# A differential-attention prompt stage on one core: score banks in turns, row maxima issued ahead of the merge

## The reference

```python
s = jnp.einsum("bqhd,bkhd->bhqk", q, k).astype(F32) * (DA_QK ** -0.5)
s = jnp.where(k_pos[None, :] <= q_pos[:, None], s, -jnp.inf)
p = jax.nn.softmax(s, axis=-1).reshape(b, DA_HEADS, 2, tq, tk)
w = p[:, :, 0] - lam * p[:, :, 1]
return jnp.einsum("bhqk,bkhd->bqhd", w.astype(v.dtype), v)
```

## Time and profile before

| | us |
|---|---|
| median of 3 runs (lowest, highest) | 2958.01 (2953.16, 2962.52) |
| the profiled execution's own time | 2952.79 |
| span of its core | 2951.1 |
| attention, from the first scores to the last output | 1342.6 to 1575 |
| PE busy, share of the span | 93% |
| DVE, ACT busy, share of the span | 46%, 22% |
| mean granted clock of PE over the span | 0.957 |

### The profile page before, as it was taken

One profiled execution on the slowest core, in us unless ns is written; L12 is line 12 of the kernel. 1 busy time (PEld: TensorE's weight loads), 2 busy tenths in 40 slices (PEclk: granted clock), 3 DMA queues, 4 the chain that ended last, 5 costly groups with the idle time before them and its releaser, 6 DMA issues.

```text
span 2951.1 us, 51413 instructions
## 1 busy us (share of the span) xinstructions
PE 2745.0 (93%) x21313; PEld 2582.2 (87%) x21313; DVE 1361.3 (46%) x1339; ACT 658.3 (22%) x967; POOL 257.1 (9%) x250
## 2 busy tenths in 40 slices
PE   6999999999999999996776999669999999999998
PEld 6999999999999999993344889439999999999998
DVE  4332233233673788776553656475453322332334
ACT  4111111112311222323322232111221111111123
POOL 1000000000000232111002454100000000000000
PEclk8999999999999999997987999769999999999999
DMA  3111111111333456669534000104211111111112
GB/s 101 50 43 50 43 50 50 43 43 50 115 99 103 143 175 223 201 188 330 164 114 124 25 28 17 42 29 145 92 44 50 50 43 45 48 50 45 48 41 74
DMA packets 270203, 252.02 MB, mean 85 GB/s; under 512 B 20724, under 2 KB 216144, under 8 KB 269920
## 3 DMA queue, kind: packets, MB, share of 16 engines
q1 hardware_dynamic: 252960, 189.42, 21.5%
q0 software_dynamic: 16896, 60.33, 5.6%
q10 hardware_dynamic: 192, 0.07, 0.0%
HBM read 209.87 MB, written 39.90 MB: 85 GB/s over the span
## 4 chain that ended last, share of the span: by engine, by line
PE 85%; DVE 9%; ACT 2%; issue 1%; DMA 1%; SPq 0%; DVEq 0%; POOL 0%; POOLq 0%; ACTq 0%
PE ps L1670 71%; DVE small L1438 1%; ACT probs L1022 1%; PE ps L1974 1%; PE ps L1989 1%; PE ps L1693 1%; PE ps L1994 1%; DVE rstd L1583 1%; PE ps L1714 1%; PE ps L1896 1%; PE ps L2001 1%; PE ps L1911 1%; PE ps L1834 1%; PE ps L2021 1%; PE ps L2029 1%
## 5 line engine op out<-in xcount | busy, mean ns | idle before, releaser
L1670 PE MATMUL ps<-h_hi,w_hi 128*128 128x344 f32 x3072 | 991.7, 323 | 10.3 <-DVE w_lo L1160 10.3
L1670 PE MATMUL ps<-h_lo,w_hi 128*128 128x344 f32 x3072 | 980.6, 319 | 0.0
L1670 PE MATMUL ps<-h_hi,w_lo 128*128 128x344 f32 x3072 | 980.3, 319 | 0.0
L1670 PEld LDWEIGHTS ps<-h_hi,w_hi 128*128 128x128 f32 x3072 | 577.8, 188 | 25.9 <-issue 19.8
L1670 PEld LDWEIGHTS ps<-h_lo,w_hi 128*128 128x128 f32 x3072 | 577.9, 188 | 2.1 <-issue 1.9
L1670 PEld LDWEIGHTS ps<-h_hi,w_lo 128*128 128x128 f32 x3072 | 577.9, 188 | 0.0
L1670 PE MATMUL ps<-ff_hi,w_hi 128*128 128x344 f32 x1056 | 337.1, 319 | 0.0
L1670 PE MATMUL ps<-ff_lo,w_hi 128*128 128x344 f32 x1056 | 336.6, 319 | 0.0
L1670 PE MATMUL ps<-ff_hi,w_lo 128*128 128x344 f32 x1056 | 336.2, 318 | 0.0
L810 ACT ACTIVATE w_hi<-w_stage 128x1024 fp32r<-128x1024 f32 x194 | 203.8, 1051 | 479.9 <-PE ps L1670 479.9
L1160 DVE TENSOR_TENSOR w_lo<-w_stage,w_hi 128x1024 fp32r<-128x1024 f32 x194 | 239.3, 1233 | 139.4 <-ACT w_hi L810 103.8
(11 more groups left out here) (388 smaller groups left out, 3219.1 us busy)
## 6 DMA issues: line engine op xcount, KB each, us to landing
w_stage<-in_ffn_up SPq DMA_DIRECT2D x176, 256.0 KB, 3.1
key_ring<-in_cache_k SPq DMA_DIRECT2D x128, 256.0 KB, 3.0
value_ring<-in_cache_v SPq DMA_DIRECT2D x128, 256.0 KB, 3.0
w_stage<-in_w_in SPq DMA_DIRECT2D x84, 256.0 KB, 3.3
w_stage<-in_ffn_down SPq DMA_DIRECT2D x80, 256.0 KB, 2.9
gate_save<-tmp POOLq DMA_DIRECT2D x16, 516.0 KB, 4.5
gate_ring<-gate_save POOLq DMA_DIRECT2D x16, 516.0 KB, 4.2
row_ring<-row_save SPq DMA_DIRECT2D x40, 128.0 KB, 2.9
```

Of the source, the lines that this page charges most:

```text
L1670: last = mm(dense[s][:, j], w[w0][:, k0 + k, :], r[:, k, j * CH:(j + 1) * CH], start=(k == 0 and n == 0), stop=(k == nk - 1 and n == 2))
```

## The change

In steps 0 to 15 two steps' scores now lie in different banks: a step's map m lies at column m x 512 + (step mod 2) x 1024, so even steps use banks 0 and 1 and odd steps 2 and 3. `scores(step)` there waits for the probabilities of the step two before instead of the one before. On DVE `maxima(step+1)` is written ahead of the merge of `step` and of the wait for its probabilities, where it stood behind the merge. In steps 16 to 31 the banks, the order and the wait of `scores` stay; `maxima` does mask, reduction and scaling for map 0, signals, and then the same for map 1 and signals again. ACT waits for one signal ahead of each map's exponential, so `neg_max` counts to 64.

```diff
@@ -135,7 +135,7 @@
     [("rstd_moved", 3), ("kk_scaled", HP), ("o_sq", HP), ("ck_u_moved", 2 * NC), ("merge_high", KT)],
     [("kk_sq", HP), ("ck_y_out", NC), ("y_moved1", 4)], [("o_root", 1), ("ck_lo_moved", NC)],
 
-    [("tok_clear", 1), ("par_moved", 2), ("lam_prod", 1), ("x_scaled", 9), ("rope_done", 8), ("z_place", ZT), ("neg_max", 32),
+    [("tok_clear", 1), ("par_moved", 2), ("lam_prod", 1), ("x_scaled", 9), ("rope_done", 8), ("z_place", ZT), ("neg_max", 64),
      ("ck_lt", NC), ("yb_full", HP), ("merge_full", KT), ("y_moved0", 5)],
     [("x_low", 9), ("vsam_made", HP), ("z_last", ZT), ("w_ready", 32), ("ck_aka", NC), ("yb_split", HP),
      ("merged", KT)],
@@ -493,6 +493,10 @@
         AKA_PS, AKR_PS, ABR_PS = [PS[:, b:b + 2, :].rearrange("p x (h n) -> p x h n", h=HP) for b in (5, 3, 5)]
         TOK_PS = [ps4(7, 0, C), ps4(7, 0, C), ps4(3, 0, C)]
         DS_PS, Y_PS = ps4(3), ps4(4, 0, C)
+
+        def score_at(step, m):
+
+            return m * 512 + step % 2 * 1024 if step < 4 * HP else m * 1024
 
         VIEW_SC = SC.rearrange("p (b g m) -> p b g m", b=NS, g=PAGES)
         VIEW_W = Wp.rearrange("p (b g h) -> p b g h", b=NS, g=PAGES)
@@ -1015,11 +1019,12 @@
 
             def probs(step):
                 s, n = step % 2, (step // HP + 1) * P
-                act.wait_ge(*ev.at("neg_max", step + 1))
                 if step >= 2:
                     act.wait_ge(*ev.at("o_done", step - 1))
                 for m in range(2):
-                    sc.activation(pr[:, s, m, 0:n], PSf[:, m * 1024:m * 1024 + n], ACT.Exp,
+                    act.wait_ge(*ev.at("neg_max", 2 * step + m + 1))
+                    b = score_at(step, m)
+                    sc.activation(pr[:, s, m, 0:n], PSf[:, b:b + n], ACT.Exp,
                                   bias=small[:, 16 + 4 * s + m:17 + 4 * s + m], scale=SCALE,
                                   accum_out=small[:, 18 + 4 * s + m:19 + 4 * s + m]).then_inc(ev["probs_made"], 1)
             probs(0)
@@ -1430,17 +1435,24 @@
             def maxima(step):
                 qi, s = step // HP, step % 2
                 n = (qi + 1) * P
-                scores = PSf[:, 0:2048].rearrange("p (m n) -> p m n", m=2)
                 dve.wait_ge(*ev.at("scores_done", step + 1))
-                diag = scores[:, :, qi * P:n]
-                in_turn(v.tensor_tensor(diag, diag, K("causal").unsqueeze(1).broadcast_to([P, 2, P]), ALU.add))
-                top = small[:, 24 + 2 * s:26 + 2 * s]
-                in_turn(v.tensor_reduce(top, scores[:, :, 0:n], AX, ALU.max))
-                in_turn(v.tensor_scalar(small[:, 16 + 4 * s:18 + 4 * s], top, -SCALE, None, ALU.mult).then_inc(ev["neg_max"], 1))
+                for ms in ((0, 1),) if step < 4 * HP else ((0,), (1,)):
+                    a, k = ms[0], len(ms)
+                    b = score_at(step, 0)
+                    scores = PSf[:, b:b + 1024].rearrange("p (m n) -> p m n", n=512)[:, :, 0:n] if k == 2 else \
+                        PSf[:, a * 1024:a * 1024 + n].unsqueeze(1)
+                    diag = scores[:, :, qi * P:n]
+                    in_turn(v.tensor_tensor(diag, diag, K("causal").unsqueeze(1).broadcast_to([P, k, P]), ALU.add))
+                    top = small[:, 24 + 2 * s + a:24 + 2 * s + a + k]
+                    in_turn(v.tensor_reduce(top, scores, AX, ALU.max))
+                    in_turn(v.tensor_scalar(small[:, 16 + 4 * s + a:16 + 4 * s + a + k], top, -SCALE, None, ALU.mult)
+                            .then_inc(ev["neg_max"], k))
             maxima(0)
             for step in range(STEPS):
                 qi, s = step // HP, step % 2
                 n = (qi + 1) * P
+                if step + 1 < 4 * HP:
+                    maxima(step + 1)
                 dve.wait_ge(*ev.at("probs_made", 2 * step + 2))
                 inv = small[:, 28 + 2 * s:30 + 2 * s]
                 in_turn(v.reciprocal(inv, small[:, 18 + 4 * s:20 + 4 * s]))
@@ -1452,7 +1464,7 @@
                 if qi >= 4:
                     dve.wait_ge(*ev.at("w_trans_hi", step + 1 - 4 * HP))
                     in_turn(v.tensor_copy(wT[s][:, 512:n], PS[:, 5, 0:n - 512]).then_inc(ev["w_hi_moved"], 1))
-                if step + 1 < STEPS:
+                if 4 * HP <= step + 1 < STEPS:
                     maxima(step + 1)
                 if step < 3:
                     sample_softmax(step)
@@ -1888,12 +1900,14 @@
             def scores(step):
                 qi, h = step // HP, step % HP
                 n = (qi + 1) * P
-                pe.wait_ge(*ev.at("probs_made", 2 * step))
+                if step >= 2:
+                    pe.wait_ge(*ev.at("probs_made", 2 * step if step >= 4 * HP else 2 * step - 2))
                 for m in range(2):
                     q = halves[m]
                     for j in range(0, n, 512):
                         w = min(512, n - j)
-                        last = mm(PSf[:, m * 1024 + j:m * 1024 + j + w], Q[q, h, qi * P:n], Kr[q, h, j:j + w],
+                        b = score_at(step, m) + j
+                        last = mm(PSf[:, b:b + w], Q[q, h, qi * P:n], Kr[q, h, j:j + w],
                                   start=True, stop=True)
                 last.then_inc(ev["scores_done"], 1)
             scores(0)
```

## The result

The changed kernel took 3,011.48 us (median of 4 runs, 3,009.81 to 3,014.50) against 2,955.59 (4 runs, 2,950.56 to 2,962.52). The ratio is 1.0188, with a 95% interval of 1.0169 to 1.0208: 55.9 us slower. The prediction said 3,000 with 2,977 to 3,018.

What follows compares the result with a forecast made beforehand. An attention chain passing between engines was taken as the bound, made serial by the change: 2,952.8 + 0.4 + 45 - 1 = 2,997, put at 3,000 us for the median's offset; 8 in 10 from 2,977 to 3,018.

Steps and rivals of the forecast that it cites:

- The serial loop: Early steps: output, filler, scores, maxima, merge, transposes, copy run in series, 7.42 us a step against 4.70 with three blocks.
- The length at either clock: Steps 4 to 14: 81.4 us for 54.9 at full PE clock (+26.5); +54 us at 1.2 GHz throughout.
- The turned sum: Early steps: a turned sum now stands in the loop, adding 1.1 us with three blocks and 1.1 with four.
- The wait of the maxima: DVE's mask instruction would wait for PE's scores in nearly all of steps 4 to 15, some 2.5 us each.
- The weight of the low clock: Steps 4 to 14: low clock weighted two thirds to 0.7, so 26.5 + 0.68 x 27.5 = +45 us.
- rival 2: Serial loop with low clock throughout and the first four steps at their bound: 3,017 us; chance 0.13.
- Steps 0 to 3: First four steps: exponentials of step 4 start 0.4 us later; taken as +0.4, bounds -1 to +5.
- Step 15: Last early step: keeps the old order, since step 16 isn't moved; no cost was added for it.
- Late steps: Steps 16 to 31: earlier exponentials gain, later sample sums lose 1.4 us at the end; net -1 us, bounds -6 to +5.
- The banks: Early scores: the second pair removes their wait for the probabilities, nearly free already: start 1395.38 instead of 1395.46.
- Splitting instructions: Late DVE maxima: by the skill's access times, three added instructions cost 0.31 us and late steps gain some 6 us more.
- Rival 3: Early steps: scores and maxima over by the probabilities' end, loop 4.04 us for 4.70, total 2,949 us; chance 0.04.

Runs made afterwards that it cites:

- e1: Kernel before with only the maxima of steps 1 to 15 moved ahead of the previous step's merge, in the old banks: 3,009.87 us, ratio 1.0189.
- e4: Changed kernel with early-step scores issued two steps ahead in PE's queue: 2,952.88 us, ratio 1.0001 to the kernel before.
- e6: Changed kernel with early scores of the next step but one issued between output and filler: 2,989.10 us, ratio 1.0112 to the kernel before.
- e5: Changed kernel with three idle 512-column matmuls added on PE in each of steps 3 to 14: 2,988.14 us, ratio 1.0098 to the kernel before.
- e3: Kernel before with only the maxima split map by map, a signal each, in steps 16 to 31: 2,953.18 us, ratio 1.0004.
- e7: Changed kernel with early scores two steps ahead, the sample's term behind the next maxima early, and split maxima only in steps 16 to 27: 2,949.36 us, ratio 0.9981.
- e2: Kernel before with only the scores in two pairs of banks in turn, maxima still behind the merge: 2,955.19 us, ratio 1.0008.

## Why the prediction was right

- **The serial loop.** Right, in its direction and in its parts. e1 shows that the hoist alone makes it, e4 that the place of the scores in PE's queue is the other half of the cause, and e6 that what stands ahead of the scores counts at nearly its full length.
- **The length at either clock.** The sums were 81.4 us for steps 4 to 14 with PE at full clock and 54 more than before, 108.9, at the low one. e5 gave 84.1 at PEclk 0.96 and the changed kernel 108.5. That the second agrees to half a us is in part luck. By its own terms, 2.5 us a step for the low clock, the sum had 34.3 us for two blocks, 40.8 for three and 33.8 for four; measured are 31.5, 41.9 and 35.1. The turned sum was taken at 1.1 us, and steps 9 and 13 took 2.2 and 2.6 us more than their neighbours.
- **The wait of the maxima.** Seen where it was said to be, but each was to be some 2.5 us, and the 11 waits of steps 4 to 14 sum to 59.3 us, 5.4 each. The prediction's own loop already gives 4.0 at full clock, from the transposes to the end of the scores; the 2.5 did not follow from it. The sum does not use it.
- **The weight of the low clock.** This is the term that was off. I gave it 0.68 and so +45 us; the measured early part is +53.5, a weight of 0.98. I had reckoned that the clock would come back in some busy stretches and help there. It came back, but at their ends, and was at 1.00 while PE waited. That is the largest part of the miss. The profiled execution is 15.8 us above the sum (60.2 longer than before, for 44.4), of which 8.5 are here, 4.1 in the late steps, 1.2 in step 15 and 2.2 outside the attention, with 0.2 the other way in steps 0 to 3; against the forecast of 3,000 the median missed by 11.5. The prediction set the low clock throughout beside its sum as the upper end, +54, and as a part of rival 2 gave it 0.13: for steps 4 to 14 that is how it came. The work in bursts shorter than the waits, which it named there, was not quite the case here: in step 10 PE worked 4.6 us and then waited 3.5.
- **Steps 0 to 3.** +0.2 us, for +0.4.
- **Step 15** was taken as unchanged, with its order, and became 1.2 us longer (6.81 for 5.64), with its output and filler at the low clock. e1, with the hoist and without the split, has 7.56, and e3, with the split alone, 4.89, so the hoist costs 1.9 there and the split gives 0.75.
- **Late steps.** The sum had 2.2 us of gain up to step 27, none behind it and 1.4 of loss, and put it as -1. Late and end together are +3.1 in the changed kernel's profile: the gain up to step 27 is there (1.1 us in this profile, 3.5 in the mean of all), and the loss at the end is 4.2 us in this profile and 4.6 in the mean of all, instead of 1.4. e7, with the split taken out of the end alone, shows where that loss sits. How it divides between DVE's later term and the loads behind it was not taken apart.
- **The banks.** Taken as worth nothing; e2 measured 1.0008.
- **Splitting instructions.** By the access times that the Trainium skill gives ("Perfetto Trace Analysis", Optimizing Scalar/DVE Operations), the estimate was some 6 us more of gain in the late steps. e3 does not bear that out: steps at nearly full clock gained what the rows gave, and over the whole kernel nothing is left (ratio 1.0004).
- **Rival 3**, faster by 9 us if the scores were early enough, was wrong for this kernel, for the reason given: its point of decision. With that point moved (e4) its loop appeared, 4.02 us for the 4.04 worked out.

## What to carry to other kernels

A second buffer lets a producer run early only if the producer's engine also issues it early: ask what stands ahead of it in that engine's queue, and move it there, before the consumer is moved ahead of other work. Moving a waiting instruction up in a queue puts everything behind it under that wait, so look for loops that pass through both queues and add up all their parts. And cost PE's work at the level at which it runs, not at the mean of the stretch: here a loop with some 3.5 us of idle PE in each step had a mean of 0.61 and all of its filler at 0.50.

## What was not expected of the hardware

- The granted clock rose at the end of PE's busy stretches and was spent on idle time: in step 10 0.50 through four of 4.6 us of work, 1.00 through most of the wait behind it, and likewise in six more of the eleven steps, so that PEclk 0.61 over a stretch went with work at 0.50 nearly throughout.
- Useless matmuls paid: 36 of 512 columns, 2.84 us a step of added work, made the changed kernel 23 us faster. The useful ones ran at 1.00 in ten of the eleven steps: in step 8 of e5 the filler took 1.04 us, where step 10 of the changed kernel has 1.89.
- The clock of a single step can differ where its code does not: step 9 was at 1.00 in the kernel before (5.10 us) and at 0.61 in e3 (8.03 us), whose early steps are unchanged.
